# A decoder layer on one core: the row mixes of the second feed-forward group move to VectorE, the differences of w_down behind them, and group 1 opens on five products of f

## The chip, the core and the metric

The kernel runs on one core of one Trainium2 chip. The metric is the device time of one execution in microseconds (us). The kernel before took 1583.93 us (median of three runs, 1583.5 to 1584.78).

A core has a matrix engine (PE, TensorE), a vector engine (DVE, VectorE), a scalar engine (ACT, ScalarE), a general engine (POOL, GpSimd) and a queue engine (SP, SyncE) that here only issues transfers (DMAs). Each engine works through its own instructions in order. Engines wait for each other on semaphores, which are counters.

## What is computed

One layer of a hybrid decoder for 1024 prompt rows and 64 sample rows (1088 rows in all, 1024 columns each): an input projection, retention heads and dilated attention heads, an output projection, and a SwiGLU feed-forward part. Only the last part is touched:

```python
h = rmsnorm(x, g_pre_ffn)
gu = h @ w_gu                                  # w_gu is 1024 x 5632
gate, up = gu[..., :D_FF], gu[..., D_FF:]      # D_FF = 2816
f = (jax.nn.silu(gate) * up) @ w_down          # w_down is 2816 x 1024
x = x + rmsnorm(f, g_post_ffn)
```

## The kernel before, in words

**Stages.** The input projection, retention and the two attentions take the first half of the time; `OutProjection` (L1635) forms the rows h of the feed-forward part until 830 us of the profiled execution, and `out_and_ffn` (L1966) does the rest. All products are made of three matmuls each: every operand is held as a high part (`_hi`, a rounding made by ACT) and a low part (`_lo`, what is left, a subtraction made mostly by DVE), and high times high, high times low and low times high are summed.

**Groups.** D_FF is worked in 11 groups of 256 columns. Group 0 is computed plainly: `first_unit(u)` on PE (L2665), for u = 0 to 5, is gate and up for one half of the group's columns (sub = u // 3) and one chunk of rows (c = u % 3; chunks of 384, 384 and 320 rows), 48 matmuls each. Unit u writes the banks `gate_ps[u % 2]` and `up_ps[u % 2]`; ACT's `unit(u)` (L2280) takes the silu of the gate, DVE's `unit(u)` (L2444) multiplies it with up and counts `f_ready`. So the banks that unit u used are free again when `f_ready` is at u + 1. Units 3 to 5 need the weight slots 4 to 7, whose low parts DVE makes with `low(n)` (L2428) after unit 0 (`lo_ready` at 8).

**Mixes of rows.** Groups 1 to 10 use Strassen's scheme with seven half-size products (P1 to P7) for the first 768 rows. It needs four combinations ("mixes") of blocks of h, each 128 x 1536 values: tile 0 is a21 + a22 (P5), tile 1 is a21 + a22 - a11 (P6), tile 2 is a21's and a11's difference (P7), tile 3 is a12 less tile 1 (P3). Each is formed as `s_sum`, then ACT rounds it to `s_hi`, and a last subtraction gives `s_lo`. Before the change DVE formed tiles 0, 1 and 3 (`sums_of_rows` L2536, `less_first_rows` L2543, `low_of_sum` L2555) and POOL formed tile 2 (`difference_of_rows` L2207 and the subtraction at L2232). The counters are `s2_formed`, `s_formed`, `s3_formed`, `s_hi_ready`, `s3_hi_ready`, `s_ready` and `s3_ready`.

**Order of group 1.** `chain(g, hh)` on PE (L2706) makes one half of a group, gate for hh = 0 and up for hh = 1. Eight weight blocks n[0] to n[7] are used in order; the chain opens with the product of n[0] into `chain_a` (= `gate_ps[0]`) and then one for the last 320 rows into `rest_ps[0]` (= `gate_ps[1]`). Before the first of them it waits for `lo_ready` (slot 8) and, in group 1, for `f_ready` at 6, that is all of group 0. Its weights come as `raw[0]` and `raw[1]`, 1 MB each, which SP loads by `load_gate_up(1, 0)` and `(1, 1)` (L2084) when `lo_ready` is at 8. ACT splits them ahead of use (`split_ahead`), DVE makes the differences of weights (`third` L2467, `fourth` L2476). After n[3] come the products for the samples, `sample_products` (L2695).

**Queues around it.** POOL, after its last low parts of h, forms tile 2, then issues four DMAs that copy keys and values of the new rows out of the z scratch (`k_prompt`, `v_prompt` of 2 MB and two small ones), then makes the low part of tile 2; later it issues copies of the caches, each released by a count of PE's products. SP's order is: w_down of group 0, the two loads of group 1, `store_t(0)` (the differences of w_down, after DVE's `differences_of_down(0)`, L2499), `store_f(0)`, the loads of group 2, and so on. Slots 8 to 13 are split on ACT and made low on DVE ahead of the group; 14 and later inside the loop over groups.

The end of the kernel multiplies f by w_down: 77 `step(s)` (L2776) and `last_product(i)`, and `finish(i)` writes the rows out.

Of the kernel before, what the change touches and what calls it, by code (L numbers as in the profile page):

```python
# [1965 lines left out]
def out_and_ffn(nc, A, z, x_mid, h, f_d, wt_d, ident, kept, inputs, w_b):  # L1966
# [16 lines left out]
    with ExitStack() as ctx:  # L1983
# [90 lines left out]
        with nc.Block() as block:  # L2074
# [127 lines left out]
            def _(pool):  # L2202
# [4 lines left out]
                def difference_of_rows():  # L2207
                    hi, lo = ((part[0, 0][:, :, :].bitcast(F32), part[0, 1][:, :, :].bitcast(F32)) for part in (h.hi, h.lo))
                    pool.tensor_tensor(s_sum[2][:, :, :], *hi, ALU.subtract).then_inc(s3_formed, 1)
                    pool.tensor_tensor(s_rest[2][:, :, :], *lo, ALU.subtract).then_inc(s3_formed, 1)  # L2210
                    pool.wait_ge(s3_formed, 2)
                    pool.tensor_tensor(s_sum[2][:, :, :], s_sum[2][:, :, :], s_rest[2][:, :, :], ALU.add).then_inc(s3_formed, 1)

# [11 lines left out]
                difference_of_rows()  # L2225
# [5 lines left out]
                pool.wait_ge(s3_hi_ready, 1)  # L2231
                pool.tensor_tensor(s_lo[2][:, :, :], s_sum[2][:, :, :], s_hi[2][:, :, :].bitcast(F32), ALU.subtract).then_inc(s3_ready, 1)  # L2232
# [14 lines left out]
            def _(act):  # L2247
# [100 lines left out]
                act.copy(s_hi[1][:, :, :], s_sum[1][:, :, :]).then_inc(s_hi_ready, 1)  # L2348
                act.wait_ge(s3_formed, 3)
                act.copy(s_hi[2][:, :, :], s_sum[2][:, :, :]).then_inc(s3_hi_ready, 1)  # L2350
                unit(3)
                split_ahead(8)
                split_ahead(9)
                split_ahead(10)
                split_ahead(11)
                act.wait_ge(s_formed, 2)
                act.copy(s_hi[0][:, :, :], s_sum[0][:, :, :]).then_inc(s_hi_ready, 1)
                unit(4)
                act.copy(s_hi[3][:, :, :], s_sum[3][:, :, :]).then_inc(s_hi_ready, 1)
# [67 lines left out]
            def _(dve):  # L2427
# [107 lines left out]

                def sums_of_rows():  # L2536
# [6 lines left out]
                def less_first_rows():  # L2543
                    a11, a11_lo = (part[0, 0][:, :, :].bitcast(F32) for part in (h.hi, h.lo))
                    a12, a12_lo = (part[1, 0][:, :, :].bitcast(F32) for part in (h.hi, h.lo))
# [3 lines left out]
                    dve.tensor_tensor(s_sum[1][:, :, :], s_rest[1][:, :, :], a11_lo, ALU.subtract).then_inc(s_formed, 1)  # L2549
                    dve.wait_ge(s_formed, 1)  # L2550
# [19 lines left out]
                sample_low_part(0, 0)  # L2570
                low_of_sum(0, 1)
                unit(3)
# [5 lines left out]
                unit(4)  # L2578
                low_of_sum(2, 3)
                differences_of_down(0)  # L2580
                unit(5)
                low(12)
                low(13)
                sample_low_part(0, 1)
# [79 lines left out]
            def _(pe):  # L2664
# [41 lines left out]
                def chain(g, hh):  # L2706
# [3 lines left out]
                    if hh:  # L2710
                        pe.wait_ge(silu_ready, 6 * g + 4)
                    else:
                        pe.wait_ge(f_ready, 6 * g if g == 1 else 6 * g - 2)
# [192 lines left out]
```

## Time and profile before

| | before |
|---|---|
| median of three runs | 1583.93 us |
| the profiled execution: its own time | 1578.07 us |
| its span, first to last instruction | 1576.3 us |
| mean granted clock of PE | 0.986 |
| busy: PE, DVE, ACT, POOL | 1490.0, 814.8, 555.7, 326.6 us |
| matmuls of group 0 (L2681) | from 830.1 to 884.1 us |

How to read it: rows of a timeline begin with the start in us from the first instruction, then the busy time in us, the engine, the line, the operation with its output and inputs, their shapes and how many instructions the row merges; in brackets stands the idle time before it and what ended it. A table by stretches gives for each engine the busy us (and number of instructions), then the mean granted clock of PE as a share of the full 2.4 GHz, the mean share of the 16 DMA engines that is busy, and GB/s. PE matmuls overlap, so the distance between two starts is what one costs.

### The profile page before, as it was taken

What the parts mean: (1) busy time and instruction counts of PE and PEld (TensorE: products, weight loads), DVE (VectorE), ACT (ScalarE), POOL (GpSimd) and SP (SyncE); (2) the same over time, 40 slices, a digit from 0 to 9 for tenths busy, and PEclk for the clock granted to TensorE, in tenths of its full rate; (3) what the DMA queues carried; (4) which work ended last, traced back from release to release, by engine and by line L of the source; (5) the groups of instructions that cost most, each with busy time, mean ns of one, the idle gap of its engine ahead of it and who ended that gap; (6) DMA issues with size and microseconds to landing.
All of it is one profiled execution on the core that took longest, in us unless ns stands there. A gap on an engine that the chain in (4) does not pass through costs nothing.

```text
span 1576.3 us, 23158 instructions
## 1 busy us (share of the span) xinstructions
PE 1490.0 (95%) x8974; PEld 1282.8 (81%) x8974; DVE 814.8 (52%) x1380; ACT 555.7 (35%) x1046; POOL 326.6 (21%) x366
## 2 busy tenths in 40 slices
PE   7999999998988888998998899999999999999996
PEld 6788888887845556766888899999999999888875
DVE  2333201104766664543557767666666675754555
ACT  4401122212144543542342433333333334544542
POOL 3245420003532334001566110100001000000001
PEclk9999999999999999999999999999999999999999
DMA  5346654527475526993464588989888894887975
GB/s 205 107 136 190 183 180 156 182 88 260 169 250 150 175 71 283 407 360 98 149 192 122 191 206 227 224 224 183 234 231 193 222 210 166 291 243 219 267 238 187
DMA packets 138253, 317.76 MB, mean 202 GB/s; under 512 B 23884, under 2 KB 65116, under 8 KB 132997
## 3 DMA queue, kind: packets, MB, share of 16 engines
q1 hardware_dynamic: 129352, 229.26, 43.6%
q0 software_dynamic: 6976, 71.32, 21.0%
q10 hardware_dynamic: 1824, 15.83, 2.4%
q8 instruction: 65, 1.06, 0.3%
q14 instruction: 36, 0.29, 0.1%
HBM read 254.45 MB, written 137.92 MB: 249 GB/s over the span
## 4 chain that ended last, share of the span: by engine, by line
PE 38%; DVE 5%; POOL 3%; DMA 3%; issue 3%; ACT 1%; SPq 1%; POOLq 0%; ACTq 0%; DVEq 0%
PE y_ps L2691 28%; PE y_ps L2773 4%; PE x_ps L2773 3%; DMA raw_step<-wt_scratch 2%; DVE slot_lo L2430 2%; POOL xm L1712 1%; DMA raw<-w_gu 1%; POOL h_lo L1726 1%; PE y_ps L2681 1%; PE y_ps L1845 1%; DVE y L1810 1%; PE m_ps L2702 1%; PE d_ps L2702 1%; DVE y L2530 1%; PE m_ps L2773 0%
## 5 line engine op out<-in xcount | busy, mean ns | idle before, releaser
L518 PE MATMUL z_ps<-w_hi,h_hi 128*128 128x512 f32 x488 | 190.6, 391 | 4.3 <-POOL h_lo L335 4.3
L518 PE MATMUL z_ps<-w_lo,h_hi 128*128 128x512 f32 x488 | 189.9, 389 | 0.0
L2691 PE MATMUL y_ps<-h_hi,slot_hi 128*128 128x320 f32 (+1 forms) x560 | 180.4, 322 | 4.7 <-DVE f L2441 4.7
L2691 PE MATMUL y_ps<-h_hi,slot_lo 128*128 128x320 f32 (+1 forms) x560 | 180.3, 322 | 0.0
L2691 PE MATMUL y_ps<-h_lo,slot_hi 128*128 128x320 f32 (+1 forms) x560 | 180.1, 322 | 0.0
L518 PE MATMUL z_ps<-w_hi,h_lo 128*128 128x512 f32 x432 | 168.1, 389 | 0.0
L131 POOL DMA_DIRECT2D ks_sample<-cache_k_win x60 | 34.3, 572 | 611.6 <-PE y_ps L2691 375.0
L2430 DVE TENSOR_TENSOR slot_lo<-raw_step,slot_hi 128x512 fp32r<-128x512 f32 x132 | 85.3, 688 | 83.5 <-ACT slot_hi L2256 83.4
L518 PEld LDWEIGHTS z_ps<-w_hi,h_hi 128*128 128x128 f32 x488 | 91.6, 188 | 24.3 <-POOL h_lo L335 4.9
L2691 PEld LDWEIGHTS y_ps<-h_hi,slot_hi 128*128 128x128 f32 x560 | 105.6, 188 | 4.9 <-issue 4.9
L2256 ACT CAST slot_hi<-raw_step 128x512 fp32r<-128x512 f32 x132 | 75.3, 618 | 93.1 <-PE y_ps L2773 34.6
L2691 PE MATMUL y_ps<-s_hi,slot_hi 128*128 128x384 f32 x320 | 107.6, 336 | 0.0
L2691 PE MATMUL y_ps<-s_hi,slot_lo 128*128 128x384 f32 x320 | 107.6, 336 | 0.0
L2691 PE MATMUL y_ps<-s_lo,slot_hi 128*128 128x384 f32 x320 | 107.5, 336 | 0.0
L518 PEld LDWEIGHTS z_ps<-w_lo,h_hi 128*128 128x128 f32 x488 | 91.6, 188 | 18.8
L2691 PEld LDWEIGHTS y_ps<-h_hi,slot_lo 128*128 128x128 f32 x560 | 105.7, 189 | 0.0
L2691 PEld LDWEIGHTS y_ps<-h_lo,slot_hi 128*128 128x128 f32 x560 | 105.6, 189 | 0.0
L430 DVE TENSOR_TENSOR w_lo<-w_raw,w_hi 128x2048 fp32r<-128x2048 f32 x14 | 31.9, 2288 | 124.1 <-ACT w_hi L365 124.1
L2430 DVE TENSOR_TENSOR slot_lo<-raw,slot_hi 128x512 fp32r<-128x512 f32 x104 | 79.8, 786 | 30.2 <-ACT slot_hi L2256 28.8
L518 PEld LDWEIGHTS z_ps<-w_hi,h_lo 128*128 128x128 f32 x432 | 81.1, 188 | 16.9
L2298 ACT COPY held<-y_ps 128x384 f32<-128x384 f32 x60 | 28.7, 479 | 119.5 <-PE y_ps L2691 119.5
L2256 ACT CAST slot_hi<-raw 128x512 fp32r<-128x512 f32 x104 | 62.1, 619 | 19.9 <-DMA raw<-w_gu 11.2
(359 smaller groups left out, 3213.2 us busy)
## 6 DMA issues: line engine op xcount, KB each, us to landing
ks_sample<-cache_k_win POOLq DMA_DIRECT2D x60, 544.0 KB, 9.2
vs_sample<-cache_v_win POOLq DMA_DIRECT2D x60, 544.0 KB, 11.3
raw<-w_gu SPq DMA_DIRECT2D x20, 1024.0 KB, 15.5
raw_step<-f_scratch SPq DMA_DIRECT2D x66, 256.0 KB, 4.0
K<-cache_k_win SPq DMA_DIRECT2D x8, 2048.0 KB
w_raw<-w_in SPq DMA_DIRECT2D x14, 1024.0 KB
z_scratch<-z_out SPq DMA_DIRECT2D x56, 256.0 KB, 2.4
raw_d<-w_down SPq DMA_DIRECT2D x11, 1024.0 KB, 13.6
```

The source lines that it names most:

```text
L131: eng.dma_start(flat(new)[:, bass.ds(row * WID, n * WID)], flat(old)[:, bass.ds(row * WID + DEC_T * WID, n * WID)]).then_inc(kept, 16)
L430: dve.tensor_tensor(w_lo[cut], w_raw[:, q], w_hi[cut].bitcast(F32), ALU.subtract).then_inc(w_lo_ready, 1)
L518: mm = pe.matmul(z_ps[t % 3][:, :], x[:, k, t * 128:t * 128 + 128], w[:, par, k, :], start=(k, n) == first, stop=(k, n) == last)
L1712: pool.tensor_tensor(self.xm[:, t % 2, :], self.y[:, :], self.inputs.x_n[:, t % 2, :], ALU.add).then_inc(self.xm_ready, 1)
L1726: pool.tensor_tensor(self.h.lo[at][cut], self.hg[:, q, :, 0:n], self.h.hi[at][cut].bitcast(F32), ALU.subtract).then_inc(self.lo_ready, 1)
L1810: dve.scalar_tensor_tensor(self.y[0:n, :], src[0:n, :], self.stat[0:n, 2:3], self.g_post[0:n, :], ALU.mult, ALU.mult).then_inc(self.y_read ...
L2256: act.copy(in_slot(slot_hi, n), source(n)).then_inc(hi_ready, 1)
L2298: act.copy(held[:, k, :], chain_a[:, 0:384]).then_inc(held_ready, 1)
L2430: dve.tensor_tensor(in_slot(slot_lo, n), source(n), in_slot(slot_hi, n).bitcast(F32), ALU.subtract).then_inc(lo_ready, 1)
L2691: mm = pe.matmul(bank[:, 0:cols], w, v[:, k, :], start=fresh and (k, m) == (0, 0), stop=(k, m) == (HK - 1, 2), skip_group_check=True)
L2702: mm = pe.matmul(sample_ps[c], f_s[:, sub, :], w[n % RING][:, :], start=(g, sub, e) == (0, 0, 0), stop=(g, sub, e) == (LAST, 1, 1), skip_g ...
L2773: mm = pe.matmul(bank, x[:, own], w[:, :], start=fresh and m == 0, stop=ends and m == 2, skip_group_check=True)
```

## The change

Tile 2 is formed on DVE: `difference_of_rows` (three subtractions or sums) between `sample_low_part(0, 0)` and `unit(3)`, and its low part in `low_of_difference` after `low_of_sum(0, 1)`. `less_first_rows` is cut in two: the second half, which forms tile 3, is now `second_rows_less` behind `unit(3)`. DVE's `unit(4)` comes ahead of `third(1, 0)`, `unit(5)` ahead of `low_of_sum(2, 3)`, and `differences_of_down(0)` goes to the end, after slots 12 and 13 and the samples' low part. On ACT the rounding of tile 2 comes after `unit(3)`, and slots 10 and 11 after `unit(4)`. POOL goes from its last low part of h to the four DMAs. On PE, `chain(1, 0)` waits for `f_ready` at 5 before its first product and at 6 before its second.

```diff
--- before.py
+++ after.py
@@ -2204,13 +2204,6 @@
                     for i in range(n, m):
                         copy_windows(pool, A, kept, i * SHARE, SHARE)
 
-                def difference_of_rows():
-                    hi, lo = ((part[0, 0][:, :, :].bitcast(F32), part[0, 1][:, :, :].bitcast(F32)) for part in (h.hi, h.lo))
-                    pool.tensor_tensor(s_sum[2][:, :, :], *hi, ALU.subtract).then_inc(s3_formed, 1)
-                    pool.tensor_tensor(s_rest[2][:, :, :], *lo, ALU.subtract).then_inc(s3_formed, 1)
-                    pool.wait_ge(s3_formed, 2)
-                    pool.tensor_tensor(s_sum[2][:, :, :], s_sum[2][:, :, :], s_rest[2][:, :, :], ALU.add).then_inc(s3_formed, 1)
-
                 def root(i):
                     t = FINAL[i]
                     pool.wait_ge(mean_ready, i + 1)
@@ -2222,14 +2215,11 @@
                 out.low(pool, PT)
                 pool.wait_ge(out.lo_ready, out.half(PT, 1))
                 out.all_stored(pool)
-                difference_of_rows()
                 for n, (p_out, s_out) in enumerate((("k_prompt", "ks_sample"), ("v_prompt", "vs_sample"))):
                     cols = slice((5 + n) * WID, (6 + n) * WID)
                     pool.dma_start(A[p_out][0, 0].rearrange("s h d -> s (h d)"), z[0:SEQ, cols]).then_inc(kept, 16)
                     pool.dma_start(A[s_out][0, :, L - DEC_T:L].rearrange("b t h d -> b t (h d)"),
                                    z[SEQ:NTOK, cols].rearrange("(b t) c -> b t c", b=DEC_B)).then_inc(kept, 16)
-                pool.wait_ge(s3_hi_ready, 1)
-                pool.tensor_tensor(s_lo[2][:, :, :], s_sum[2][:, :, :], s_hi[2][:, :, :].bitcast(F32), ALU.subtract).then_inc(s3_ready, 1)
                 for g in range(1, LAST):
                     for hh in range(2):
                         pool.wait_ge(done, made(g, hh, 1))
@@ -2346,16 +2336,16 @@
                 sample_high(0, 0)
                 act.wait_ge(s_formed, 1)
                 act.copy(s_hi[1][:, :, :], s_sum[1][:, :, :]).then_inc(s_hi_ready, 1)
+                unit(3)
                 act.wait_ge(s3_formed, 3)
                 act.copy(s_hi[2][:, :, :], s_sum[2][:, :, :]).then_inc(s3_hi_ready, 1)
-                unit(3)
                 split_ahead(8)
                 split_ahead(9)
-                split_ahead(10)
-                split_ahead(11)
                 act.wait_ge(s_formed, 2)
                 act.copy(s_hi[0][:, :, :], s_sum[0][:, :, :]).then_inc(s_hi_ready, 1)
                 unit(4)
+                split_ahead(10)
+                split_ahead(11)
                 act.copy(s_hi[3][:, :, :], s_sum[3][:, :, :]).then_inc(s_hi_ready, 1)
                 unit(5)
                 split_ahead(12)
@@ -2533,6 +2523,17 @@
                     dve.wait_ge(x_landed[i % 2], 16 * (i // 2) + 16)
                     dve.tensor_tensor(y[t][rows, :], y[t][rows, :], x_m[i % 2][rows, :], ALU.add).then_inc(y_ready, 1)
 
+                def difference_of_rows():
+                    hi, lo = ((part[0, 0][:, :, :].bitcast(F32), part[0, 1][:, :, :].bitcast(F32)) for part in (h.hi, h.lo))
+                    dve.tensor_tensor(s_sum[2][:, :, :], *hi, ALU.subtract).then_inc(s3_formed, 1)
+                    dve.tensor_tensor(s_rest[2][:, :, :], *lo, ALU.subtract).then_inc(s3_formed, 1)
+                    dve.wait_ge(s3_formed, 2)
+                    dve.tensor_tensor(s_sum[2][:, :, :], s_sum[2][:, :, :], s_rest[2][:, :, :], ALU.add).then_inc(s3_formed, 1)
+
+                def low_of_difference():
+                    dve.wait_ge(s3_hi_ready, 1)
+                    dve.tensor_tensor(s_lo[2][:, :, :], s_sum[2][:, :, :], s_hi[2][:, :, :].bitcast(F32), ALU.subtract).then_inc(s3_ready, 1)
+
                 def sums_of_rows():
                     (a21, a22), (a21_lo, a22_lo) = ((part[0, 1][:, :, :].bitcast(F32), part[1, 1][:, :, :].bitcast(F32)) for part in (h.hi, h.lo))
                     dve.tensor_tensor(s_sum[0][:, :, :], a21, a22, ALU.add).then_inc(s2_formed, 1)
@@ -2542,11 +2543,13 @@
 
                 def less_first_rows():
                     a11, a11_lo = (part[0, 0][:, :, :].bitcast(F32) for part in (h.hi, h.lo))
-                    a12, a12_lo = (part[1, 0][:, :, :].bitcast(F32) for part in (h.hi, h.lo))
                     dve.wait_ge(s2_formed, 3)
                     dve.tensor_tensor(s_rest[1][:, :, :], s_sum[0][:, :, :], a11, ALU.subtract).then_inc(s2_formed, 1)
                     dve.wait_ge(s2_formed, 4)
                     dve.tensor_tensor(s_sum[1][:, :, :], s_rest[1][:, :, :], a11_lo, ALU.subtract).then_inc(s_formed, 1)
+
+                def second_rows_less():
+                    a12, a12_lo = (part[1, 0][:, :, :].bitcast(F32) for part in (h.hi, h.lo))
                     dve.wait_ge(s_formed, 1)
                     dve.tensor_tensor(s_rest[3][:, :, :], a12, s_sum[1][:, :, :], ALU.subtract).then_inc(s2_formed, 1)
                     dve.wait_ge(s2_formed, 5)
@@ -2568,20 +2571,23 @@
                 unit(2)
                 less_first_rows()
                 sample_low_part(0, 0)
+                difference_of_rows()
+                unit(3)
+                second_rows_less()
                 low_of_sum(0, 1)
-                unit(3)
+                low_of_difference()
+                unit(4)
                 third(1, 0)
                 for n in range(8, 12):
                     low(n)
                 fourth(1, 0)
                 low_of_sum(1, 0)
-                unit(4)
+                unit(5)
                 low_of_sum(2, 3)
-                differences_of_down(0)
-                unit(5)
                 low(12)
                 low(13)
                 sample_low_part(0, 1)
+                differences_of_down(0)
                 for g in range(1, GROUPS):
                     for i in range(8):
                         low_ahead(gate_up(g, 0, i) + LEAD)
@@ -2710,8 +2716,10 @@
                     if hh:
                         pe.wait_ge(silu_ready, 6 * g + 4)
                     else:
-                        pe.wait_ge(f_ready, 6 * g if g == 1 else 6 * g - 2)
+                        pe.wait_ge(f_ready, 6 * g - (1 if g == 1 else 2))
                     product(n[0], chain_a, moving[P1], True)
+                    if c == 0:
+                        pe.wait_ge(f_ready, 6)
                     product(n[0], rest_ps[0], first_rows[0, 2], True)
                     pe.wait_ge(lo_ready, n[1] + 1)
                     if c:
```

## Rows read from the trace of the kernel before

**Rows 1.** The span by stretches: us, busy of PE, PEld, DVE, ACT, POOL, clock, DMA.

```profile
854.70:858.70 4.00, 0.22 (x2) 0.00 (x0) 4.00 (x3) 0.44 (x1) 4.00 (x3) 0.97 0.00 0
858.70:862.00 3.30, 3.24 (x10) 3.27 (x11) 3.30 (x2) 0.00 (x0) 1.68 (x3) 0.52 0.81 258
...
884.40:889.10 4.70, 0.05 (x2) 0.08 (x1) 4.63 (x8) 1.62 (x5) 0.00 (x0) 1.00 0.38 142
889.10:892.00 2.90, 2.90 (x10) 2.90 (x11) 1.75 (x4) 0.61 (x2) 0.00 (x0) 0.52 1.02 383
...
902.30:947.60 45.30, 45.30 (x274) 44.97 (x273) 29.86 (x54) 16.66 (x34) 4.40 (x8) 1.00 0.79 194
```

**Rows 2.** Timeline of PE, single matmuls: start, busy, line, operation, idle before.

```profile
843.74 0.33 PE L2681 MATMUL y_ps<-h_lo,slot_hi 128*128 128x384 f32 x1
...
847.73 0.31 PE L2681 MATMUL y_ps<-h_hi,slot_hi 128*128 128x320 f32 x1
...
854.61 0.31 PE L2681 MATMUL y_ps<-h_hi,slot_lo 128*128 128x320 f32 x1
858.76 0.66 PE L2681 MATMUL y_ps<-h_hi,slot_hi 128*128 128x384 f32 x1 [3.84 <-DVE slot_lo L2430]
...
884.09 0.31 PE L2681 MATMUL y_ps<-h_hi,slot_lo 128*128 128x320 f32 x1
889.05 0.53 PE L2691 MATMUL y_ps<-h_hi,slot_hi 128*128 128x384 f32 x1 [4.65 <-DVE f L2441]
...
902.22 0.39 PE L2702 MATMUL m_ps<-slot_hi,f_s 128*128 128x512 f32 x1
```

**Rows 3.** Timeline of POOL from its mix to the low part of tile 2.

```profile
846.04 3.84 POOL L2209 TENSOR_TENSOR s_sum<-h_hi 128x1536 f32<-128x1536 f32 x1
...
853.89 3.76 POOL L2212 TENSOR_TENSOR s_sum<-s_sum,s_rest 128x1536 f32<-128x1536 f32 x1
857.60 0.85 POOL L2228 DMA_DIRECT2D k_prompt<-z_scratch  x1
...
870.69 3.96 POOL L2232 TENSOR_TENSOR s_lo<-s_sum,s_hi 128x1536 fp32r<-128x1536 f32 x1 [10.32 <-ACT s_hi L2350]
```

**Rows 4.** Timeline of DVE from the low parts of slots 4 to 7.

```profile
845.60 12.60 DVE L2430 TENSOR_TENSOR slot_lo<-raw,slot_hi 128x512 fp32r<-128x512 f32 x4 [0.99 <-ACT slot_hi L2256]
...
858.58 1.75 DVE L2538 TENSOR_TENSOR s_sum<-h_hi 128x1536 f32<-128x1536 f32 x1
...
863.71 0.54 DVE L2441 TENSOR_TENSOR f<-silu,y_ps 128x128 f32<-128x128 f32 x2
...
871.22 3.52 DVE L2449 TENSOR_TENSOR f_s<-f,f_s 128x64 fp32r<-128x64 f32 x1
874.66 1.75 DVE L2557 TENSOR_TENSOR s_lo<-s_sum,s_hi 128x1536 fp32r<-128x1536 f32 x1
876.33 0.54 DVE L2441 TENSOR_TENSOR f<-silu,y_ps 128x384 f32<-128x384 f32 x1
...
883.57 0.55 DVE L2441 TENSOR_TENSOR f<-silu,y_ps 128x384 f32<-128x384 f32 x1
```

**Rows 5.** Line 2430 from 844 to 859 us: duration in ns, minimum, median, maximum.

```profile
L2430 DVE TENSOR_TENSOR slot_lo<-raw,slot_hi x4: 908/3958/4004, 845.6 to 854.3; 128x512 fp32r<-128x512 f32 x4
```

**Rows 6.** Timeline of ACT: silu of unit 2, first split of slot 8.

```profile
854.96 0.44 ACT L2284 ACTIVATE silu<-y_ps 128x320 f32<-128x320 f32 x1 [6.54 <-PE y_ps L2681]
...
876.95 1.14 ACT L2256 CAST slot_hi<-raw 128x512 fp32r<-128x512 f32 x2 [5.96 <-DMA raw<-w_gu]
```

**Rows 7.** SP's timeline: the two loads of group 1.

```profile
858.23 1.05 SPq L2090 DMA_DIRECT2D raw<-w_gu  x2
```

**Rows 8.** Landing of those two loads.

```profile
DMA to landing us min/median/max: 18.7/20.5/22.2
```

**Rows 9.** Landing of all 20 loads of line 2090.

```profile
DMA to landing us min/median/max: 5.0/15.5/22.7
```

**Rows 10.** PE's waits from 905 us to the end: total us, times, longest.

```profile
PE x_ps L2773 <- DVE slot_lo L2430: 3.9, 2, 3.3
```

## The prediction

> **What bounds the kernel now.** I read the span by stretches first, then the timeline of PE, then for each idle stretch of PE the timeline of the engine that ended it. From 902.3 us to the end of the groups PE is busy all the time at a granted clock of 1.00 [rows 1], and from 905 us to the end its waits for another engine come to little, 3.9 us on the largest line [rows 10]. So time is to be won there only by fewer matmuls, and the change removes none. Around the change it is otherwise: PE stands still twice. Unit 2's last matmul starts at 854.61, the next could start 0.15 us later, and unit 3 starts at 858.76, released by DVE's slot_lo. Unit 5's last starts at 884.09, and group 1 starts at 889.05, released by DVE's f [rows 2]. After each halt the granted clock is 0.52 for some 3 us, which is the lower level, 1.2 GHz [rows 1]; ten to twelve matmuls run there at half speed.
>
> Why does DVE release them so late? **The first halt:** the low parts of slots 4 to 7 take 12.60 us for four instructions [rows 4]; one takes 0.91, the others about 4.0 us [rows 5]. An undisturbed one should take a third of the 1.75 us of a 128x1536 one [rows 4], 0.6 us. Beside them POOL forms tile 2: three instructions of 3.8 to 4.0 us from 846.04 to 857.65 [rows 3]. Each slow low ends as a POOL instruction ends. DVE meets the same again at 871.22, where a 128x64 subtraction takes 3.52 us [rows 4] beside POOL's L2232, 870.69 to 874.65 [rows 3]. I read this as exclusion: a DVE instruction with both inputs in SBUF stands while a POOL instruction that reads SBUF runs.
>
> The Trainium skill says so too ("SBUF — State Buffer", section "Who interferes with whom"): whichever of the two starts first has the shared ports for its whole instruction, and the other fully blocks. By that rule the lows fall to their own length once POOL is quiet, and the sum is the one below; by the opposite, that DVE's own operands slow it, rival 3's time results. The trace agrees with the page: 4.0 us beside POOL's 3.8 to 4.0.
>
> **The second halt:** group 1 waits for `f_ready` at 6. Behind the first halt DVE is never idle: it forms the mixes, loses 3.5 us to POOL, and runs `third`, lows 8 to 11, `fourth`, three `low_of_sum` and the four differences of w_down ahead of the last f. ACT's splits begin at 876.95, when raw[0] lands [rows 6], 18.7 us [rows 8] after SP's issue at 858.23 [rows 7], which itself waited for the slow lows.
>
> **The change, part by part.** I lay out the new timeline. All until 845.60 stays.
>
> *POOL's work leaves.* POOL loses 11.6 us and 4.0 us of mixing [rows 3]; it was on nobody's path except by the exclusion. Its four z copies are issued from about 846 instead of 857.60. DVE's lows: the first 0.9 (POOL's last low part of h is still running), three more at 0.6: slots 4 to 7 are done at 848.3 instead of 858.2. PE needs them at 854.76. **First halt gone: 4.0 us, and with it the slow clock.** The slow stretch costs 10 matmuls of 0.32 instead of 0.17, 1.5 us.
>
> *DVE takes it up.* Four instructions of 128x1536 at 1.75 us [rows 4], 7.0 us more. f(1) at 848.45; the three of `sums_of_rows` end at 854.1; f(2) waits for the silu of unit 2, whose rows don't move (854.96 + 0.44 [rows 6]): 855.45. From f at 863.71 to the sample's low part at 871.22 lie f and four mixes, 7.51 us [rows 4]; two mixes are half of it, so the sample's low part is at 859.4, tile 2's three end at 864.8 (5.2 us), and f(3), whose gate PE ended at 863.1 (below), starts at 864.65. Tile 3's two, `low_of_sum(0, 1)` and `low_of_difference` take 4 x 1.75 and a little: 872.0. f(4)'s gate is out of PE at 871.5 and of ACT at 872.0: f(4) starts at 872.05. From f to f with `third`, lows 8 to 11, `fourth` and one `low_of_sum` between, the trace has 883.57 - 876.33 = 7.24 us [rows 4]. The same set stands between f(4) and f(5): f(5) starts at 879.3 and ends at 879.85; its silu is ready at 879.15.
>
> *PE.* A 384-row matmul costs (847.73 - 843.74) / 23 = 0.1735 us, a 320-row one (854.61 - 847.73) / 47 = 0.1464 [rows 2]. Units 3 and 4 take 8.33 each, unit 5 takes 7.03: from 854.76 to 863.1, 871.4 and 878.45. Group 1's first product needs `f_ready` 5 (872.6) and slot 8's low part (874.7): it starts at 878.45. It takes 12 x 0.1735 = 2.1, so `f_ready` 6 is wanted at 880.55 and there at 879.85. **That slack is 0.7 us, the thinnest of all.** With the wait left as it was, PE would stand 1.4 us at 878.45: this is what the edit on PE is worth. Second halt gone: 889.05 - 884.24 = 4.8 us, and 1.7 us of slow clock.
>
> *The loads.* SP issues at 848.3 instead of 858.23. With the 18.7 us [rows 8] raw[0] lands at 867.0. ACT wants it after tile 2's rounding, 866.3; slots 8 and 9 take 1.14 [rows 6], tile 0's rounding waits for tile 3 anyway (868.7), and silu 4 at 871.5 is met if raw[0] lands by 869.6 or so. The moved z copies now have 2.4 us head start over the loads instead of 0.6, since they follow the last low part of h while the loads follow the lows; both ends: 5.0 us for a load in an idle system and 22.7 us for the longest [rows 9]. I take 18.7, the row with the same neighbours, and keep 22.7 + 1.8 as the far end.
>
> A rule of the Trainium skill bears on these copies ("SBUF — State Buffer", section "SBUF: two separate sides"): transfers issued from GpSimd can be held back while VectorE runs in a two-port mode. Here they would stand beside DVE's subtractions. By that rule the copies would start late, the loads would have the DMA engines to themselves, the sum would be the same and rival 2 would have hardly a chance. No row of before settles it.
>
> *Put last.* `differences_of_down(0)` ends at 885.5, 7 us after PE's start of the group instead of before it. Behind it stand low 14, low 15 (886.7) and the first gate sum (887.2); then ACT makes slot 16, DVE its low part at 889.4. PE wants slots 14 and 15 at 890.0 and slot 16 at 891.9. Hidden, with 2.5 us to spare. SP's `store_t(0)`, `store_f(0)` behind it go out at 885 to 889, and the load of group 2 behind them is released only by low 23. `low_of_difference` waits for ACT's rounding (866.3): no wait.
>
> **The sum.** From 854.76 to the samples' products at 902.22 [rows 2] are 47.5 us. New: 8.33 + 8.33 + 7.03 + 36 x 0.1735 + 36 x 0.1464 = 35.2 us. **Gain 12.2 us**, which agrees with 4.0 + 1.5 + 4.8 + 1.7 = 12.0. Behind it every issue is released by PE or by DVE that keeps up, so all shifts. The profiled span goes from 1576.3 to 1564.1, its execution from 1578.07 to 1565.9. The runs shown have a median 5.9 us above the profiled one; I take the same microseconds off: 1583.93 - 12.2 = **1571.7 us**.
>
> **The rivals.**
> 1. *The forecast*, 1571.7, own range 1569 to 1574.
> 2. *raw[0] lands late.* At 848.3 + 24.5 = 872.8: slots 8 and 9 and tile 0's rounding delay silu 4 to 875.4; f(5) ends at 883.8, 3.3 us after PE wants it, with perhaps 0.5 more before. Gain 8.4, **1575.5**. For it: the head start of the copies; against: the traffic is the same.
> 3. *The lows stay slow*, because something else slows them. The first halt stays; DVE then has f(2) at 863.7, f(3) at 872.9, f(4) at 880.3, f(5) done at 888.1, while PE wants it at 886.3: 1.8 us left of the second halt's 6.5. Gain 4.7, **1579.2**. Against: [rows 3, 5].
> 4. *The gain is taken back behind it.* The DMA engines are busy 0.79 while PE is full [rows 1]; had they a backlog that PE's earlier pace runs into, the steps at the end would wait. Within 0.2%, say **1582**. Against: PE waits for nothing in the groups [rows 10].
> 5. *Slower.* The loads fall behind the z copies. Each us of landing past 869.6 costs PE one, and a halt of 4 us a slow clock on top (1.7). The 12.2 us are gone when raw[0] lands 31 to 32 us after its issue; at 38 us it lands at 886.3: 16.7 + 1.7 - 12.2 = 6.2 us slower, **1590.1**. Against: 22.7 us is the longest of 20 [rows 9].
>
> **How the numbers follow.** Chances: forecast 0.77, late load 0.10, slow lows 0.04, taken back 0.06, slower 0.03. Faster by over 0.2% (3.2 us, about what can be told from no change): 0.77 + 0.10 + 0.04 = 0.91; within: 0.06; slower: 0.03. Range: the forecast's own and the late load's, 1568.5 to 1576; below 1569 only if the runs' longer time holds longer halts than the profiled one.
>
> **What would show it.** The four L2430 beside 846 us at 0.6 to 0.9; no idle of PE between 830 and 905 over 0.3 us; clock 1.00 from 855 on; the first matmul of L2691 at 878 to 879, the samples' at 890; raw[0] landing by 869. Wrong would be: an idle before the second product of group 1 (f not ready), ACT waiting past 870 for raw, or the copies' rows later than 850.

## The result, and the profile after

| | before | after |
|---|---|---|
| median of the first six runs | 1584.82 us (1583.5 to 1587.74) | 1567.05 us (1561.12 to 1573.55) |
| ratio, 95% interval | | 0.9893 (0.9869 to 0.9917) |
| the profiled execution, its own time | 1578.07 us | 1566.13 us |
| its span | 1576.3 us | 1564.3 us |
| mean granted clock of PE | 0.986 | 0.990 |

The kernel became faster, by 17.8 us between these medians. The forecast was 12.2 us and 1571.7 us, with a range down to 1568.5: the six runs' median lies 1.45 us below that end. The profiled span was forecast at 1564.1 us and is 1564.3, which is close partly by luck: in the kernel after, unit 0 starts 0.67 us earlier and the end part takes 0.65 us longer than before, and both scatter by several us from one execution to the next (table below). What the working inside the trace can be held to is the stretch that the change touches: forecast 12.2 us shorter, measured 11.9. What failed is that the range left no room for the scatter of the runs. The sections below look at both.

The span by stretches, kernel after: us, then busy us (and instructions) of PE, PEld, DVE, ACT, POOL, then the granted clock, DMA share, GB/s.

```profile
854.70:858.70 4.00, 4.00 (x25) 4.00 (x24) 3.91 (x5) 0.27 (x2) 0.00 (x0) 1.00 0.95 313
858.70:862.00 3.30, 3.30 (x20) 3.30 (x19) 3.30 (x4) 1.49 (x1) 0.00 (x0) 1.00 1.03 343
862.00:878.30 16.30, 16.30 (x103) 16.30 (x102) 15.72 (x17) 7.64 (x10) 0.00 (x0) 1.00 0.33 107
878.30:882.00 3.70, 3.70 (x25) 3.70 (x24) 3.70 (x6) 3.07 (x7) 0.00 (x0) 1.00 0.00 0
882.00:890.00 8.00, 8.00 (x51) 7.96 (x50) 6.37 (x12) 2.93 (x7) 1.09 (x2) 1.00 0.66 199
890.00:935.00 45.00, 45.00 (x273) 44.71 (x272) 30.65 (x55) 16.55 (x34) 4.30 (x8) 1.00 0.92 218
```

Where PE stood still or ran at the lower clock in [rows 1], it is now busy all the time from 854.7 to 935 us, and the clock is 1.00 throughout. PE's timeline, kernel after, against [rows 2]:

```profile
853.93 0.31 PE L2687 MATMUL y_ps<-h_hi,slot_lo 128*128 128x320 f32 x1
854.09 0.34 PE L2687 MATMUL y_ps<-h_hi,slot_hi 128*128 128x384 f32 x1
...
878.09 0.34 PE L2697 MATMUL y_ps<-h_hi,slot_hi 128*128 128x384 f32 x1
...
880.18 0.31 PE L2697 MATMUL y_ps<-h_hi,slot_hi 128*128 128x320 f32 x1
...
889.63 0.39 PE L2708 MATMUL m_ps<-slot_hi,f_s 128*128 128x512 f32 x1
```

Unit 3 follows unit 2 at the usual distance, group 1 starts at 878.09 (forecast 878.45), the samples' products at 889.63 (forecast 890.0; all of this execution is 0.67 us early from before unit 2). POOL, DVE, ACT and SP of the kernel after, one fence per engine:

```profile
845.60 0.85 POOL L2220 DMA_DIRECT2D k_prompt<-z_scratch  x1 [0.30 <-POOL h_lo L1726]
```

```profile
844.93 2.73 DVE L2420 TENSOR_TENSOR slot_lo<-raw,slot_hi 128x512 fp32r<-128x512 f32 x4 [0.99 <-ACT slot_hi L2246]
...
863.95 0.55 DVE L2431 TENSOR_TENSOR f<-silu,y_ps 128x384 f32<-128x384 f32 x1
...
871.77 0.55 DVE L2431 TENSOR_TENSOR f<-silu,y_ps 128x384 f32<-128x384 f32 x1 [0.47 <-ACT silu L2274]
...
878.86 0.54 DVE L2431 TENSOR_TENSOR f<-silu,y_ps 128x128 f32<-128x128 f32 x2
```

```profile
866.54 1.14 ACT L2246 CAST slot_hi<-raw 128x512 fp32r<-128x512 f32 x2 [0.99 <-DMA raw<-w_gu]
```

```profile
847.68 1.26 SPq L2090 DMA_DIRECT2D raw<-w_gu  x2
```

The four lows take 2.73 us instead of the 12.60 of [rows 4]. The f of units 3, 4 and 5 start at 863.95, 871.77 and 878.86, forecast (less the 0.67 us) 863.98, 871.38 and 878.63. raw[0] lands at 866.5, that is 18.8 us after its issue.

### The profile page after: what moved, and what is told of

Its sections match the earlier page's. It is cut to its first block, busy times and chain, and to the rows that moved or that the text cites. A ratio compares the mean times of both kernels' runs of the same rounds, so it can differ in the third digit from the quotient of the medians.

```text
span 1564.3 us, 23158 instructions
## 1 busy us (share of the span) xinstructions
PE 1484.0 (95%) x8974; PEld 1276.5 (82%) x8974; DVE 808.6 (52%) x1384; ACT 555.9 (36%) x1046; POOL 310.4 (20%) x362
## 4 chain that ended last, share of the span: by engine, by line
PE 41%; POOL 4%; DVE 3%; issue 3%; DMA 2%; ACT 1%; SPq 1%; POOLq 0%; ACTq 0%; DVEq 0%
PE y_ps L2697 28%; PE y_ps L2781 4%; PE y_ps L2687 3%; PE x_ps L2781 3%; DMA raw_step<-wt_scratch 2%; POOL xm L1712 1%; POOL h_lo L1726 1%; DVE slot_lo L2420 1%; PE y_ps L1845 1%; DVE y L1810 1%; PE m_ps L2708 1%; PE d_ps L2708 1%; DVE y L2520 1%; PE m_ps L2781 0%; PE d_ps L2781 0%
## 5 line engine op out<-in xcount | busy, mean ns | idle before, releaser
L518 PEld LDWEIGHTS z_ps<-w_lo,h_hi 128*128 128x128 f32 x488 | 91.6, 188 | 18.8
L2420 DVE TENSOR_TENSOR slot_lo<-raw,slot_hi 128x512 fp32r<-128x512 f32 x104 | 69.9, 691 | 30.1 <-ACT slot_hi L2246 28.8
```

The lines of the kernel that those rows point to most:

```text
L518: mm = pe.matmul(z_ps[t % 3][:, :], x[:, k, t * 128:t * 128 + 128], w[:, par, k, :], start=(k, n) == first, stop=(k, n) == last)
L2420: dve.tensor_tensor(in_slot(slot_lo, n), source(n), in_slot(slot_hi, n).bitcast(F32), ALU.subtract).then_inc(lo_ready, 1)
```

## The experiments

A run of the whole kernel turned out to scatter by several us, so most readings below are taken from one stretch of a profile: **from unit 0's first matmul to the first product for the samples**. It holds all that the change touches. These are the starts and spans that the profiles show, in us:

| kernel | unit 0 starts | to group 1 | to the samples' products | from there to the steps with w_down | from there to the end | span |
|---|---|---|---|---|---|---|
| before | 830.1 | 58.9 | 72.1 | 441.2 | 232.8 | 1576.3 |
| again_before | 834.9 | 58.8 | 72.0 | 441.2 | 234.6 | 1582.8 |
| after | 829.4 | 48.6 | 60.2 | 441.2 | 233.5 | 1564.3 |
| again_after | 823.2 | 48.7 | 60.2 | 441.2 | 235.3 | 1559.9 |
| third_after | 835.3 | 48.7 | 60.2 | 441.2 | 235.5 | 1572.2 |
| dve_only | 831.3 | 54.0 | 68.3 | 441.2 | 234.1 | 1574.9 |
| pool_reads | 831.5 | 54.2 | 67.3 | 441.5 | 235.4 | 1575.7 |
| pool_writes | 829.1 | 48.7 | 60.2 | 441.2 | 237.1 | 1567.7 |
| pool_one | 834.0 | 48.7 | 60.7 | 441.5 | 236.6 | 1572.9 |
| full_wait | 830.5 | 50.1 | 61.7 | 441.2 | 234.1 | 1567.5 |
| down_only | 832.7 | 48.7 | 62.2 | 441.2 | 237.1 | 1573.2 |
| down_first | 831.7 | 48.7 | 66.5 | 441.2 | 236.5 | 1576.0 |
| before_late_copies | 833.3 | 58.8 | 71.9 | 459.9 | 233.8 | 1598.9 |
| after_late_copies | 831.0 | 48.7 | 60.2 | 463.3 | 235.0 | 1589.4 |

pool_one, down_only, before_late_copies and after_late_copies were executed once each, so for them there is no interval, and the stretch is all that they are read by.

### Both kernels drawn again: again_before, again_after, third_after

No edit.

> The kernel before, unchanged, as a second draw. The prediction took the profiled execution (1578.07 us) as a true picture of the runs (median 1584.8 us) and the 12.2 us worked out on it as the gain of the runs. Theory A: the profiled execution was a fortunate draw of stretches far from the change; then a new profile shows both halts of PE at 854 to 889 us with the same lengths (4.0 and 4.8 us), and its other time is spread before 815 us. Theory B: the halts themselves are longer in most executions (the loads land later, POOL's mixes take longer); then a new profile with a span near 1583 us shows halts that are longer by some 5 us in sum. Ratio to the kernel before: 1.000.

> The changed kernel, unchanged, as a second draw. Theory A: the gain is 12 us, so the ratio comes out near 0.9923, and the first interval (0.9869 to 0.9917) was off by the spread of the draws. Theory B: the ratio stays at 0.989 (17 us). In either case the stretch from 815 us to the samples' products has the length of the first profile of it within 0.3 us.

> The changed kernel, a third draw. The two draws so far gave ratios of 0.9893 and 0.9925, while the stretch from unit 0 to the samples' products was 60.2 us in both profiles against 72.1 and 72.0 before (11.9 us, ratio 0.9925). Theory A (the gain is the local one, the rest is spread of the draws): ratio 0.992 to 0.993, stretch 60.2 us. Theory B (about 5 us more are won where no profile so far shows it): ratio 0.989 to 0.990 again.

Measured: again_before 1583.58 us median of 12 runs (1575.57 to 1588.04), ratio 0.9999 (0.9979 to 1.0019). again_after 0.9925 (0.9901 to 0.9949), third_after 0.9925 (0.9905 to 0.9944). The stretch is 72.1 and 72.0 us before, 60.2 us in all three draws after. Its 11.9 us are a ratio of 0.9925. Theory B is out on both counts: the profile of again_before has a span of 1582.8 us, near the runs' median, and its halts are not longer. PE's waits in that profile, after 815 us (total us, times, longest):

```profile
PE y_ps L2691 <- DVE f L2441: 4.4, 1, 4.4
PE y_ps L2681 <- DVE slot_lo L2430: 3.8, 1, 3.8
```

What differs between executions is the way to unit 0, which has the same code in all of them: it starts between 823.2 and 835.3 us. The end part takes 232.8 to 237.1 us. The stretch 357 to 435 us (retention) in the kernel after, first and second draw:

```profile
357.00:435.00 78.00, 69.01 (x578) 61.73 (x578) 49.84 (x97) 15.57 (x28) 35.03 (x22) 0.93 0.60 204
```

```profile
357.00:435.00 78.00, 70.33 (x593) 60.25 (x592) 55.08 (x105) 16.21 (x29) 36.19 (x23) 0.98 0.66 221
```

In the second draw the granted clock is 0.98 instead of 0.93 there, and the last matmul of retention starts at 428.7 instead of 433.5 us. So the granted clock of this stage goes with the one execution that is far ahead of the others. It doesn't order the rest: in the thirteen other profiles the same stretch has 0.91 or 0.93, and unit 0 starts at 829.1 to 834.0 us with 0.91 and at 829.4 to 835.3 us with 0.93. What sets the clock in one execution and not in another, and what makes up the rest of the scatter, is open.

Taken together, 18 runs of the kernel after have a median of 1570.2 us (mean 1569.4, standard deviation 4.2) and 51 runs of the one before, made beside them, 1583.1 us (mean 1582.9, standard deviation 3.0; the 12 runs of again_before aren't among them). The means differ by 13.5 us; by these deviations that is known to about 2 us, so it does not differ from 11.9. The expectation of again_after counts its stretch from 815 us, which is no fixed point, since unit 0 itself starts 6.3 us earlier there; counted from unit 0 the two profiles agree to 0.03 us.

### POOL beside DVE: pool_reads, pool_one, pool_writes

pool_reads gives POOL its three instructions back, and DVE overwrites the result (`pool_over` is a counter added for it):

```diff
                 out.all_stored(pool)
+                hi, lo = ((part[0, 0][:, :, :].bitcast(F32), part[0, 1][:, :, :].bitcast(F32)) for part in (h.hi, h.lo))
+                pool.tensor_tensor(s_sum[2][:, :, :], *hi, ALU.subtract).then_inc(pool_over, 1)
+                pool.tensor_tensor(s_rest[2][:, :, :], *lo, ALU.subtract).then_inc(pool_over, 1)
+                pool.wait_ge(pool_over, 2)
+                pool.tensor_tensor(s_sum[2][:, :, :], s_sum[2][:, :, :], s_rest[2][:, :, :], ALU.add).then_inc(pool_over, 1)
...
                 def difference_of_rows():
+                    dve.wait_ge(pool_over, 3)
```

> The changed kernel, but POOL also forms tile 2 at its old place, into the same tiles, and DVE forms it again over it later (the result is DVE's). This brings back POOL's three reading instructions alone. My theory: the lows of slots 4 to 7 take 12.6 us again, the first halt is back with 4.0 + 1.5 us, the loads go out 10 us later, f(5) is done at 887.5 while PE wants it at 885.7: 7.3 us slower than the changed kernel, span 1571.6. Rival (it was the ACT splits or the DMA that slowed the lows): the lows stay at 2.7 us and the span at 1564.3.

pool_one keeps only the first of the three (and waits for one):

> The changed kernel, but POOL does the first of its three reading instructions (128x1536, 3.8 us) beside the lows of slots 4 to 7; DVE overwrites the result later. Theory of exclusion by whole instructions: one low stands for the POOL instruction's length (about 4.0 us), the other three take 0.6 to 0.9; they are done 3.3 us later than in the changed kernel, still ahead of unit 3, so the first halt does not come back: stretch 60.2 us. Rival (a shared rate while POOL reads): two or more lows are stretched in part. In either case the loads go out 3.3 us later and raw[0] lands at 870, which is the edge of what I worked out as slack (869.6): up to 0.5 us on the stretch.

pool_writes has three fills in their place:

```diff
+                for own in (s_sum[2], s_rest[2]):
+                    pool.memset(own[:, :, :], 0.0).then_inc(pool_over, 1)
+                pool.wait_ge(pool_over, 2)
+                pool.memset(s_sum[2][:, :, :], 0.0).then_inc(pool_over, 1)
```

> The changed kernel, but POOL fills tile 2's two places with zeros three times (128x1536 each) where it once formed tile 2; DVE overwrites them later. POOL writes SBUF and reads nothing. Theory (only a POOL instruction that reads SBUF excludes DVE's two-input subtractions): the lows of slots 4 to 7 stay at 0.6 to 0.9 us each, stretch 60.2 us. Rival (any POOL instruction does, or shares the write side): the lows are stretched to the length of the fills, and with them the first halt comes back by as much as the fills last beyond 854 us.

The line of the lows of slots 4 to 7 (ns: minimum, median, maximum), first pool_reads, then pool_one, then pool_writes:

```profile
L2426 DVE TENSOR_TENSOR slot_lo<-raw,slot_hi x4: 920/3954/4002, 847.0 to 855.7; 128x512 fp32r<-128x512 f32 x4
```

```profile
L2423 DVE TENSOR_TENSOR slot_lo<-raw,slot_hi x4: 677/798/3996, 849.5 to 854.9; 128x512 fp32r<-128x512 f32 x4
```

```profile
L2425 DVE TENSOR_TENSOR slot_lo<-raw,slot_hi x4: 679/680/908, 844.6 to 846.6; 128x512 fp32r<-128x512 f32 x4
```

Three reading instructions stretch three lows to 4.0 us; one stretches one. POOL's row beside it in pool_one:

```profile
849.98 3.84 POOL L2220 TENSOR_TENSOR s_sum<-h_hi 128x1536 f32<-128x1536 f32 x1
```

Three fills of 1.38 us each, at the same place, stretch none. The first two of them, in pool_writes, beside lows that run from 844.6 to 847.3 us:

```profile
845.00 1.38 POOL L2220 MEMSET s_sum<- 128x1536 f32 x1
846.32 1.38 POOL L2220 MEMSET s_rest<- 128x1536 f32 x1
```

So a POOL subtraction that reads SBUF keeps DVE's two-input subtraction out for its whole length, and a POOL fill, which reads nothing, doesn't. That it is the reading, and not something else in which a fill differs from a subtraction, is the likely cause, but not shown by these runs. pool_reads costs 7.1 us on the stretch (expected 7.3), with a halt of 3.85 us, the lower clock after it, and 1.3 us ahead of the second product of group 1:

```profile
860.19 0.66 PE L2694 MATMUL y_ps<-h_hi,slot_hi 128*128 128x384 f32 x1 [3.85 <-DVE slot_lo L2426]
889.27 0.42 PE L2704 MATMUL y_ps<-h_hi,slot_hi 128*128 128x320 f32 x1 [1.26 <-DVE f L2437]
```

The ratios by the runs: pool_reads against the kernel before 0.9961 (0.9939 to 0.9983); pool_writes 0.9928 (0.9907 to 0.9950).

pool_one costs 0.5 us, the upper end of what was expected, but not for the reason expected. raw[0] landed late enough that ACT waited 2.1 us for it, and the sixth f was 0.3 us late for PE; between the two stands DVE, and DVE never waited. The stretch from 855.50 to 884.60 us of pool_one (DVE is the third engine):

```profile
855.50:884.60 29.10, 29.10 (x178) 29.10 (x178) 28.93 (x28) 11.07 (x15) 1.05 (x2) 1.00 0.67 224
```

From the f of unit 1 (855.50) to the last f (884.61) DVE goes from one instruction to the next. It came out of the lows 3.1 us later than in the kernel after (21.5 instead of 18.3 us behind unit 0's start), caught up the 1.8 us that it stands idle there (1.30 ahead of the f of unit 2, 0.47 ahead of that of unit 4), and starts the last f 1.2 us later than there (50.6 instead of 49.4 us), which is more than its slack of 0.8. So the run confirms that thin slack, and says nothing of the slack of the loads.

### The engine without the order: dve_only

DVE forms tile 2, POOL doesn't, and all else stays in the order of before:

```diff
                 sample_low_part(0, 0)
+                difference_of_rows()
                 low_of_sum(0, 1)
+                low_of_difference()
                 unit(3)
```

> Tile 2 is formed on VectorE in the place of DVE's old order between the samples' low part and the low part of tile 1; nothing else is moved, PE still waits for all of f, w_down's differences stay ahead of the last f. My theory (POOL excludes DVE): the four lows of slots 4 to 7 take 2.7 us, the first halt goes. DVE's order then makes f(3) at 871.1, f(4) at 878.3, f(5) done at 883.7 us: a halt of PE of 0.9 us ahead of unit 5 and one of about 5 us ahead of group 1, with a slow clock of 1.6 us after it. Sum: some 7 us slower than the changed kernel, 5 us faster than before, span 1571.5. Rival (the order does the work, the engine does not matter): as slow as before or slower, since DVE has 7 us more to do ahead of f.

Measured: stretch 68.3 us, ratio 0.9963 (0.9944 to 0.9983). Group 1's first matmul and the stretches around it:

```profile
885.33 0.66 PE L2694 MATMUL y_ps<-h_hi,slot_hi 128*128 128x384 f32 x1 [4.65 <-DVE f L2431]
```

```profile
880.60:885.30 4.70, 0.08 (x1) 0.00 (x1) 4.63 (x8) 1.54 (x4) 0.00 (x0) 0.89 0.37 136
885.30:889.00 3.70, 3.67 (x12) 3.70 (x13) 1.83 (x4) 0.68 (x2) 0.00 (x0) 0.50 0.87 324
```

So the engine alone, in the old order, is worth 72.1 - 68.3 = 3.8 us, and the new order (on DVE, ACT and PE together) the other 8.1 us. The first halt is gone (the one ahead of unit 5 is 0.3 us, expected 0.9), the second has its old length of 4.65 us, and the lower clock lasts 5.8 us behind it instead of 3.5, which costs 2.7 us instead of 1.6. So 8.1 us were lost where 7.2 were expected. The rival, which saw no gain in the engine, is out.

### The order, part by part: full_wait, down_only, down_first

full_wait undoes the edit on PE:

```diff
-                        pe.wait_ge(f_ready, 6 * g - (1 if g == 1 else 2))
+                        pe.wait_ge(f_ready, 6 * g if g == 1 else 6 * g - 2)
```

> The changed kernel with the one edit on PE undone: group 1 waits for all six products of f before its first matmul. In the profile of the changed kernel the first product starts at 878.09 us and the sixth f is done at 879.40. My theory: PE stands 1.3 to 1.4 us ahead of group 1, the clock stays at 1.00, stretch from unit 0 to the samples' products 61.5 us instead of 60.2. Rival (the wait costs nothing, since the samples' products or slot 16 are late anyway): 60.2 us.

Measured: stretch 61.7 us, a halt of 1.3 us, and the clock stays. The first matmul of group 1:

```profile
880.62 0.41 PE L2697 MATMUL y_ps<-h_hi,slot_hi 128*128 128x384 f32 x1 [1.29 <-DVE f L2431]
```

The edit on PE is worth 1.5 us. Its ratio by the runs was 0.9895 (0.9874 to 0.9916), lower than the 0.9925 of the later draws of the kernel with the edit, though the stretch is longer: the runs can't tell 1.5 us, the stretch can.

down_first puts the low part of tile 3 and the four differences of w_down back ahead of the last f; down_only moves the differences alone and leaves `low_of_sum(2, 3)` where the change has it. down_first:

```diff
+                low_of_sum(2, 3)
+                differences_of_down(0)
                 unit(5)
-                low_of_sum(2, 3)
                 low(12)
                 low(13)
                 sample_low_part(0, 1)
-                differences_of_down(0)
```

> The changed kernel with only w_down's four differences put back ahead of DVE's last f of group 0 (2.66 us); the low part of tile 3 stays behind it. The last f is done 52.7 us after unit 0's start, PE wants it at 50.8: a halt of 1.9 us. So far halts of 1.3 us left the clock at 1.00 and one of 3.4 us was followed by 5.6 us at the lower clock, which cost 2.6. Stretch 62.1 us if the clock stays, 63.5 to 64.8 if it falls. Rival (DVE has room): 60.2.

> The changed kernel with w_down's four differences and the low part of tile 3 put back ahead of DVE's last f of group 0. They are 1.67 + 2.66 us of DVE. My theory: f is done at 883.7 us instead of 879.4, PE wants it at 880.2: a halt of 3.6 us ahead of group 1's second product, and if the clock falls for it as it did after 3.8 and 4.7 us, 1.5 us more; stretch 63.8 to 65.3 us. Rival (DVE has room there): 60.2 us.

Measured: 62.2 us in down_only and 66.5 us in down_first, whose ratio is 0.9950 (0.9925 to 0.9975). In down_only PE waits 1.8 us ahead of the second product, and in down_first 3.4 us:

```profile
885.35 0.41 PE L2697 MATMUL y_ps<-h_hi,slot_hi 128*128 128x320 f32 x1 [1.77 <-DVE f L2431]
```

```profile
886.02 0.63 PE L2697 MATMUL y_ps<-h_hi,slot_hi 128*128 128x320 f32 x1 [3.44 <-DVE f L2431]
```

In down_only the clock stays at 1.00. In down_first the stretches behind the halt are

```profile
886.00:889.50 3.50, 3.48 (x13) 3.48 (x14) 2.51 (x5) 1.66 (x4) 0.00 (x0) 0.50 0.95 352
889.50:893.00 3.50, 3.50 (x16) 3.50 (x15) 0.22 (x1) 0.00 (x0) 1.09 (x2) 0.68 0.18 60
```

From 886.02 to about 891.7 us the matmuls run at half rate. Of the 6.3 us that down_first loses, 3.6 are the later start of the second product, and the other 2.7 are the clock, above the 1.5 expected. So DVE work put ahead of the last f costs PE nearly its whole length past a slack of 0.8 us, and the halt of 3.4 us cost three quarters as much again by the clock. Of the 8.1 us of the new order this accounts for the parts around the last f; the earlier f of units 3 and 4 and the new order on ACT weren't undone by themselves.

### Was the load on the path: before_late_copies, after_late_copies

The four z copies wait for a later count of PE; in the kernel before they come behind tile 2's low part as well:

```diff
+                pool.wait_ge(done, made(1, 0, 5))
                 for n, (p_out, s_out) in enumerate((("k_prompt", "ks_sample"), ("v_prompt", "vs_sample"))):
```

> The kernel before, but POOL's four z copies (4.25 MB) wait for group 1's sixth product, behind the low part of tile 2. They no longer share the DMA engines with the two loads of group 1, so raw[0] should land 5 to 9 us after its issue instead of 18.7. The chain of waits of the kernel before charges 18.7 us to this load. Theory (DVE's own order is what ends last; it has work in hand all through that time): stretch from unit 0 to the samples' products stays at 72.1 us. Rival (the load is on the path, as the chain says): the stretch is shorter by as much as the second halt and its slow clock allow, 4.8 to 6.5 us, so 65.6 to 67.3 us.

> The changed kernel with the same delay of the four z copies. raw[0] should land at 853 to 857 us instead of 866.5. My theory: nobody waits for it either way, stretch 60.2 us; ACT's idle of 1.0 us ahead of the split of slot 8 goes, and nothing follows from it. Rival (the landing is on the path with no slack): the stretch shortens by up to 1 us.

The two loads landed 5.1 to 7.9 us after their issue, instead of 18.7 to 22.2, and the stretch stayed: 71.9 against 72.1 us, 60.2 against 60.2. So the load was **not** on the path, though the chain of waits of the kernel before follows it for 18.70 us: DVE had other work in hand through all of that time, and its own order ended last. The landing of the two loads, before_late_copies and after_late_copies:

```profile
DMA to landing us min/median/max: 5.1/6.4/7.6
```

```profile
DMA to landing us min/median/max: 5.4/6.7/7.9
```

Elsewhere the delayed copies did harm that no theory had named: the groups took 459.9 and 463.3 us instead of 441.2. In after_late_copies the copies are issued at 891.94 us and the first load of group 2 at 893.77. PE, the stretch and ACT:

```profile
935.33 0.66 PE L2698 MATMUL y_ps<-s_hi,slot_hi 128*128 128x384 f32 x1 [20.44 <-ACT held L2289]
```

```profile
905.00:920.00 15.00, 9.89 (x63) 9.62 (x61) 3.00 (x6) 1.00 (x2) 2.15 (x4) 0.93 1.08 236
920.00:935.00 15.00, 0.00 (x0) 0.00 (x0) 0.16 (x1) 0.81 (x2) 0.00 (x0) 0.50 0.92 165
```

```profile
934.19 0.62 ACT L2247 CAST slot_hi<-raw 128x512 fp32r<-128x512 f32 x1 [27.78 <-DMA raw<-w_gu]
```

PE stands 20.4 us; the release is put down to ACT's `held`, but ACT itself stood 27.8 us for a load of w_gu with the DMA engines at 0.92 to 1.08. That load landed 40.4 us after its issue; in the kernel after the loads of group 2 take 21.0 us at most. POOL works in order, so two copies of the caches (0.5 MB each) were held back with the four and came right behind them. Together they cost 18.7 and 22.1 us at this place. Why the engines moved so few bytes there (165 GB/s at a share of 0.92) isn't shown. The change moves the copies the other way, to an earlier time, where no wait for them is seen.

## Why the prediction was right and wrong

**Wrong: the scatter of the runs, put at nothing.** The step that failed is the range, and in it the sentence "below 1569 only if the runs' longer time holds longer halts than the profiled one". The gain was taken off the median of three runs within 1.3 us of each other, as if such a median came out the same each time, and no term of the range stood for the scatter. Two numbers at hand spoke against it: the profiled execution was 5.4 us below the lowest of the three runs, and the prediction's own time for the profiled execution after, 1565.9 us (measured 1566.13), lay below its range.

What the runs showed in its place: executions lie between 1575.15 and 1587.74 us in 51 runs before and between 1561.12 and 1574.69 in 18 after. A median of six of the latter is uncertain by about 2 us (4.2 us x 1.25 / the root of 6). And times below 1569 came without any difference in the halts: the three profiled executions of the kernel after have spans of 1559.9, 1564.3 and 1572.2 us, and the same stretch of 60.2 us without a halt.

The median of all 18 runs is 1570.2 us, 1.5 us from the forecast and inside the range; the first six had 1567.05. That these six were a low draw fits, but isn't proven: their mean is 3.2 us below that of the other twelve, with an uncertainty of about 2 us on the difference. The first interval (to 0.9917), which excludes the 0.9925 of the two later draws, fits the same scatter. The step "I take the same microseconds off" is borne out, since the means differ by 13.5 us, known to about 2, and the stretch by 11.9; no gain beyond the local one was found, since the groups have the same length as before. It was luck that the three runs at hand were close to the many: their median was 1583.93 and that of the 51 is 1583.1.

**Right, point by point.**
- *The exclusion* (12.6 us for four lows): 2.73 us after, and pool_reads (three stretched), pool_one (one stretched) and pool_writes (none) bring it back, dose it and leave it out. Rival 3 is out.
- *The first halt*, 4.0 us and 1.5 of slow clock: gone. It comes back as 3.85 us in pool_reads.
- *The new timeline of DVE*: f(3), f(4) and f(5) off by 0.0, 0.4 and 0.2 us.
- *The second halt*, 4.8 and 1.7 us: gone. The sum was 12.2 us, the stretch gave 11.9. The rest is the price of a 384-row matmul, read from unit 1 as 0.1735 us: in units 3 and 4 they are 0.1767 us apart, which is 96 x 0.0032 = 0.3 us.
- *The slack of the sixth f*, 0.7 us: 880.18 - 879.40 = 0.8 us. full_wait priced the edit on PE at 1.5 us (forecast 1.4).
- *The load*: landed 18.8 us after issue, at no cost. Rivals 2 and 5 did not happen. How late it may land was worked out (869.6 us) and not tested: in pool_one, with the loads out 3.3 us later, ACT waited for it, but DVE, which was behind by its own work, didn't wait for ACT.
- *w_down's differences put last*: nobody waits for them. Put back, they cost 2.0 us.
- *What lies behind*: 441.2 us in the groups in both kernels. Rival 4 is out.
- *The Trainium skill on the z copies* ("SBUF — State Buffer", "SBUF: two separate sides"): the page warns that VectorE's two-port modes starve transfers issued from GpSimd. The prediction asked whether this would hold back the copies here. They were issued at 845.6 us beside DVE's subtractions, and the DMA engines were at 0.98 from 848 to 850 us; no holding back is seen. The page's later section "Who interferes with whom" has `tensor_tensor`, which is what these subtractions are, as an operation without a two-port mode and as not stalling DMA. So the rule didn't bear on them, and the trace agrees. Its other rule there, that VectorE with two SBUF inputs is kept out only by a GpSimd instruction that reads SBUF, agrees with pool_reads (4.0 us) and pool_writes (0.68 us).

```profile
848.00:850.00 2.00, 2.00 (x16) 2.00 (x15) 2.00 (x3) 0.00 (x0) 0.38 (x1) 1.00 0.98 346
```

**Left open:** what sets the granted clock of the retention stage in one execution or another, and what makes the start of unit 0 scatter by 12 us; whether the chip has a part in it (the two later draws were made on two chips); and whether the 1.6 us between the difference of the means (13.5) and the stretch (11.9) is anything but scatter.

## What to carry to other kernels

Before taking three close runs as a base, hold the profiled execution against them: if they differ by more than the runs do among each other, the kernel scatters, the range must take that in, and small effects are read from a stretch with fixed ends in the profile rather than from the whole. Work given to GpSimd because it is idle isn't free: here each of its instructions that reads SBUF stood in the way of VectorE's two-input instructions for its whole length, and work on the engine that feeds TensorE belongs in the order in which TensorE asks for it. A load that the chain of waits follows isn't thereby on the path: where the waiting engine has other work in hand, its landing costs nothing; delay or hasten it once before believing it.

## What the runs showed of the hardware that I had not expected

- The time at the lower clock after a halt of PE isn't fixed: 3.0 us after the halt of 3.8 us before unit 3 in the kernel before and 3.5 us after that of 4.65 us before group 1, but 5.7 us after one of 3.4 us in down_first and 5.8 us after one of 4.65 us in dve_only. In the cost, 1.5 to 2.7 us. Halts of 1.3 and 1.8 us left the clock at 1.00.
- The granted clock of the retention stage was 0.98 in one execution and 0.91 to 0.93 in the thirteen others, read in the same stretch, with nothing changed in the code of that stage.
- The same 4.25 MB of copies cost nothing beside group 0 (the stretch is 60.2 us with them there and without), and issued some 45 us later they cost, with the two copies held back behind them, 22.1 us.
